# One row's gate matmuls moved from the boundary between two tiles into the middle of the second

## What is computed

```python
def _mixer_rglru(x, h0, conv_buf, p):
    gate_br, rnn_br = jnp.split(x @ p['w_in_c'], 2, axis=-1)
    xc, new_buf = _causal_dwconv(rnn_br, conv_buf, p['conv_w_c'], p['conv_b_c'])
    xb = xc.reshape(bsz, length, N_LRU_BLOCKS, LRU_BLOCK)
    r = sigmoid(einsum('blnc,ncd->blnd', xb, p['w_gate_a']) + p['b_gate_a'])
    i = sigmoid(einsum('blnc,ncd->blnd', xb, p['w_gate_x']) + p['b_gate_x'])
    log_a = LRU_C * r * log_sigmoid(p['lru_lambda'])
    a = exp(log_a)
    b = sqrt(-expm1(2.0 * log_a)) * (i * xc)
    _, h = associative_scan(_linear_combine, (a, b), axis=1)
    y = gelu(gate_br) * h
    return y @ p['w_out_c'], h[:, -1], new_buf
```

## Time and profile before

| what | value |
|---|---|
| median of 3 runs | 1378.18 us |
| lowest, highest | 1377.60, 1379.18 us |
| profiled execution, its own time | 1379.3 us |
| its span, first to last instruction | 1377.5 us |
| PE, DVE, ACT, POOL busy | 1354.0, 957.2, 721.3, 137.7 us |

### The profile page before, as it was taken

How to read it: one execution, slowest core, us unless ns; L and a number is a source line. 1 busy time by engine, 2 the same in 40 slices (tenths; PEclk the granted TensorE clock), 3 DMA queues, 4 the chain that set the end, 5 groups by cost and what they waited for, 6 DMA issues and landing times.

```text
span 1377.5 us, 24827 instructions
## 1 busy us (share of the span) xinstructions
PE 1354.0 (98%) x9860; PEld 1328.7 (96%) x9860; DVE 957.2 (69%) x1499; ACT 721.3 (52%) x1129; POOL 137.7 (10%) x146
## 2 busy tenths in 40 slices
PE   7999999999999999999999999999999999999996
PEld 7999999999999999999999999999999999999996
DVE  5657566565788658844886778888884688448865
ACT  5443544453565347722764568755652467236734
POOL 0020111100230000000000330022400000000002
PEclk9999999999999999999999999999999999999998
DMA  8165587849812345533554259853498855335522
GB/s 313 62 227 190 138 191 190 255 105 286 220 59 69 89 130 161 169 95 100 162 163 141 77 187 209 227 133 103 141 222 234 247 161 176 92 115 161 169 62 85
DMA packets 80899, 217.47 MB, mean 158 GB/s; under 512 B 6928, under 2 KB 9232, under 8 KB 80528
## 3 DMA queue, kind: packets, MB, share of 16 engines
q1 hardware_dynamic: 52704, 138.95, 30.9%
q0 software_dynamic: 27648, 76.03, 22.7%
q10 hardware_dynamic: 432, 0.91, 0.2%
HBM read 208.23 MB, written 74.74 MB: 205 GB/s over the span
## 4 chain that ended last, share of the span: by engine, by line
PE 87%; DVE 7%; ACT 3%; DMA 1%; issue 1%; SPq 0%; DVEq 0%; ACTq 0%
PE PS L781 27%; PE PS L782 26%; PE PS L783 26%; DMA raw<-weights 1%; PE PS L950 1%; PE PS L959 1%; DVE Y L1891 1%; PE PS L965 1%; PE PS L909 1%; DVE Y L1879 1%; PE PS L930 1%; DVE S L2220 1%; PE PS L939 1%; PE PS L1096 0%; DVE wlo L1598 0%
## 5 line engine op out<-in xcount | busy, mean ns | idle before, releaser
L781 PE MATMUL PS<-xhi,whi 128*128 128x296 f32 (+1 forms) x1536 | 470.3, 306 | 7.8 <-DVE wlo L1604 7.6
L782 PE MATMUL PS<-xlo,whi 128*128 128x296 f32 (+1 forms) x1536 | 458.8, 299 | 0.0
L783 PE MATMUL PS<-xhi,wlo 128*128 128x296 f32 (+1 forms) x1536 | 458.5, 298 | 0.0
L1130 ACT ACTIVATE whi<-raw 128x1024 fp32r<-128x1024 f32 (+2 forms) x256 | 254.3, 995 | 198.7 <-PE PS L783 192.9
L1598 DVE TENSOR_TENSOR wlo<-raw,whi 128x1024 fp32r<-128x1024 f32 (+2 forms) x256 | 294.2, 1152 | 64.9 <-ACT whi L1130 55.6
L781 PEld LDWEIGHTS PS<-xhi,whi 128*128 128x128 f32 x1536 | 290.9, 189 | 10.8 <-issue 8.2
L782 PEld LDWEIGHTS PS<-xlo,whi 128*128 128x128 f32 x1536 | 291.4, 190 | 1.4
L783 PEld LDWEIGHTS PS<-xhi,wlo 128*128 128x128 f32 x1536 | 290.4, 189 | 0.0
L781 PE MATMUL PS<-hhi,whi 128*128 128x296 f32 (+2 forms) x864 | 258.1, 299 | 0.4 <-DVE Y L1816 0.4
L782 PE MATMUL PS<-hlo,whi 128*128 128x296 f32 (+2 forms) x864 | 256.9, 297 | 0.0
L783 PE MATMUL PS<-hhi,wlo 128*128 128x296 f32 (+2 forms) x864 | 256.2, 297 | 0.0
(11 more groups left out here) (268 smaller groups left out, 1674.5 us busy)
## 6 DMA issues: line engine op xcount, KB each, us to landing
raw<-weights SPq DMA_DIRECT2D x118, 512.0 KB, 4.3
weight_sums<-weights POOLq DMA_DIRECT2D x24, 2048.0 KB, 16.7
raw<-weights SPq DMA_DIRECT2D x100, 256.0 KB, 3.3
weight_sums<-weight_sums POOLq DMA_DIRECT2D x8, 2048.0 KB, 10.6
raw<-weight_sums SPq DMA_DIRECT2D x64, 256.0 KB, 3.4
raw<-weight_sums SPq DMA_DIRECT2D x32, 512.0 KB, 4.1
raw<-weights SPq DMA_DIRECT2D x16, 384.0 KB, 3.3
Y<-xT SPq DMA_DIRECT2D x8, 296.0 KB, 10.6
```

The lines of the kernel that those rows point to most:

```text
L781: pe.matmul(dst, wh, h, start=first, stop=False, skip_group_check=onto)
L782: pe.matmul(dst, wh, lo, start=False, stop=False, skip_group_check=onto)
L783: return pe.matmul(dst, wl, h, start=False, stop=last, skip_group_check=onto)
L1130: act.activation(high(u, i)[:, 0:n], raw_of(u, i), ACT.Copy).then_inc(w_hi, 1)
```

## The change

The gates of the eighth row (m = 7) leave `GATES_AFTER`, where they stood behind index 13. `GATES_WITHIN` names index 14, k step 3 and row 7: `gemm` for index 14 is given a side function that issues `gates(7)` behind the fourth k step, so 24 of the tile's matmuls stand in front of the gates and 24 behind. `GATES_READ` is written so that its entry for index 14 is again row 7. No instruction is added or removed.

```diff
-GATES_AFTER = {3: (0, 1), 5: (2,), 6: (3,), 9: (4,), 10: (5,), 12: (6,), 13: (7,)}
-GATES_READ = {i if i == 3 else i + 1: rows for i, rows in GATES_AFTER.items()}
+GATES_AFTER = {3: (0, 1), 5: (2,), 6: (3,), 9: (4,), 10: (5,), 12: (6,)}
+GATES_WITHIN = (14, 3, 7)
+GATES_READ = {i if i == 3 else i + 1: rows for i, rows in GATES_AFTER.items()} | {GATES_WITHIN[0]: GATES_WITHIN[2:]}
...
+            def gates_within(u, k):
+                if k == GATES_WITHIN[1]:
+                    gates(GATES_WITHIN[2])
+
             first_tiles(U_RNN, 1)
             pe.wait_ge(gw_loaded, 16)
             for i in range(3, len(MIXER)):
-                gemm(U_RNN + i, xhi, xlo)
+                gemm(U_RNN + i, xhi, xlo, side=gates_within if i == GATES_WITHIN[0] else None)
                 for m in GATES_AFTER.get(i, ()):
                     gates(m)
```

## The result

| kernel | median of 11 runs | lowest, highest |
|---|---|---|
| before | 1378.19 us | 1377.60, 1380.68 us |
| after | 1381.58 us | 1379.31, 1382.50 us |

The ratio is 1.0017 with a 95% interval of 1.0009 to 1.0024: slower by about 2.3 us, inside the 0.2% that I had called no change, but outside the measurement's own uncertainty. The forecast was +0.66 us. The ratio compares means; the medians lie further apart, 3.4 us (1.0025), because the runs of after fall into two groups and the median lies in the upper one. That median, 1381.58, is 0.3 above the upper end of my range; 1378.18 times the ratio, 1380.5, lies inside it, but above 1380.2, where the range of my sum alone had ended.

A forecast was written before the change was run, and what follows sets the result against it. TensorE, busy 98%, was taken to bound the kernel, with a chain from the eighth row's gates to accumulator 0 ending equally late. +0.73 - 0.07 = +0.66 us on 1378.18 gave 1378.8 us, range 1377.4 to 1381.3.

The forecast's parts named there:

- (a): Before the fifteenth tile: TensorE's wait goes, as the tile's own needs are already met; gain 2.36 us.
- (b): Eighth row's gates inside the fifteenth tile: start 0.83 us later, end 0.73 late; 0 to 0.4 extra for their place.
- (c): After the gates, the tile's other half and the sixteenth tile: TensorE free at 908.91, 2.47 us earlier.
- (d): ScalarE and VectorE chain behind the gates: 0.73 us later, so the output projection starts at 912.21 after a 3.30 us wait.
- (e): Second output tile: the sixteenth tile's gelu follows the other at once, so a wait of 0.07 us is saved.
- (f): Output pair's seventh k step, needing the fourth pair of recurrent rows: both ends move 0.73 us, slack of 1.7 stays.
- The sum: Whole kernel: chain delay of 0.73 us less 0.07 saved at the second output tile, +0.66 us.
- Rival 2: New pause before the output projection: the clock falls, costing up to 3.1 us, 1381.9 us; chance 0.17.
- Rival 1: Output projection: not held by accumulator 0, so TensorE keeps 1.0 us of its gain, 1377.2 us; chance 0.07.
- rival 3: Fifteenth tile's first half or the moved gates meet another wait: 1378.2 to 1381.4 us; chance 0.03.

The follow-up runs named there:

- before_look3: The kernel before, unedited, in a further profiled execution: 1379.13 us.
- k5: The changed kernel with the gates behind the sixth k step instead of the fourth: median 1382.86 us, ratio 1.0026 to the kernel before.
- fill5: The changed kernel with five unneeded f32 matmuls in the pause before the output projection: median 1379.13 us, ratio 1.0009 to the kernel before.
- before_look1: The kernel before, unedited, in another profiled execution: 1378.74 us.
- before_look2: The kernel before, unedited, in a further profiled execution: 1380.2 us.
- k2: The changed kernel with the gates behind the third k step instead of the fourth: median 1379.82 us, ratio 1.0008 to the kernel before.
- k1: The changed kernel with the gates behind the second k step instead of the fourth: median 1378.00 us, ratio 0.9995 to the kernel before.
- k2_fill3: k2 with three unneeded f32 matmuls in the pause before the output projection: median 1378.63 us, ratio 0.9998 to the kernel before.
- k3_early_w: The changed kernel with ScalarE's weight conversion for unit 17 moved ahead of its gate reads: median 1382.07 us, ratio 1.0026 to the kernel before.

## Why the prediction was right and wrong

- **(a), (b), (c)** held to 0.01 us: no pause at 894, gates 897.35, PE free at 908.92. Nothing was to be added for gates inside an accumulation (1.77 us to the next matmul in both places), the lower end of my 0 to 0.4.
- **(d)** held, in place and in size: output projection at 912.20, pause 3.1 us by records, released by the gelu. The reading that a start 0.14 us behind a gelu is a wait, though no view named it, was the one that mattered; before_look3 names the wait, and in k5 both ends of the chain move together, by 1.59 (gates) and 1.60 us (output projection).
- **(e)** held in mechanism: the gelus follow each other. The first stretch of the projection is 0.15 shorter than in the profile of before (13.28 in fill5 against 13.43), where I counted 0.07. But before_look1 and before_look3 have 13.30 and 13.27: there the gelus followed each other already, and nothing was to be saved.
- **(f)** held: no profile of after shows a wait at the seventh k step.
- **The sum**, +0.66, was a term too small. It took the delay of the gates from the one profile in which the convolution ended latest; with the two other undisturbed profiles it is 0.86 and 1.12, with nothing to take off by (e). fill5, which has the late chain and no fall, measured 1.0009 (1.0000 to 1.0018), that is 1.2 us.
- **Rival 2**, the clock, was right in mechanism, place and price (3.1 us at most; measured 1.3 to 2.8), and wrong in its chance. The failed step is "decides from a pause somewhere between the 2.2 us that were harmless and the 2.3 to 2.8 us that were not". Harmless was what one execution showed. The pause at the same place, shorter with 1.97 us, wasn't harmless in before_look2, and 2.29 us at 910 wasn't in k2. A pause of about 2 us has a chance of a fall (about 3 in 10 in before, 6 of 11 in k2), one of 3.1 a larger one (15 of the 22 runs of after have a mean clock of 0.996 or less), one of 4.7 left no execution below 1381.44. With the median of after more often than not in a disturbed group, 0.17 should have been near one half, and the likeliest time near 1380.5.
- **Rival 1** fell with (d), **rival 3** with (a).

Together: 2.3 us by the ratio. The starts put the chain at 0.6 to 1.1 us and the rest is the clock, net of the falls that before has as well and after loses with its pause at 894. The split isn't sharper than that, as the interval of fill5 alone is 2.5 us wide. That the time by the ratio lies in the stated range is owed to the room that I left toward rival 2, and so is luck as far as the sum is concerned: the range of the sum alone ended at 1380.2.

## What to carry to other kernels

Before you move work behind a wait to fill a pause, follow what that work feeds: if it leads back to the engine that paused, filling the pause with something in front of it makes the chain later and collects the pause again, larger, at the chain's end. Look for that end by starts, not by idle time, since overlapping records hid 0.1 us here. And where TensorE pauses for about 2 us or more, as it did here, count a fall of the clock with a chance, not as something that one profile rules out. Splitting the pause (k1) or filling it with matmuls that nobody needs (fill5, k2_fill3) took the falls away.

## What the runs showed of the hardware

- A fall before the output projection cost 1.3, 1.5, 2.1, 2.5 and 2.8 us in five profiles, 0.45 of the time that matmuls ran at the low level, and the same kernel has executions with none. The cost can't be told from the pause's length: 3.1 us gave 2.8 in one profile and 1.3 in another, and 4.7 us gave 2.1, since part of the low level passed in the pause.
- Matmuls that nobody needs can pay: with 2.5 us of them in a pause of 3.1 no run exceeded 1379.99, where 4 of 11 had exceeded 1382.2 (ratio 1.0009 and 1.0018, intervals that overlap).
- The same convolution ended between 10.05 and 10.67 us after the same point of PE's program over all profiles, and between 10.09 and 10.67 in the four of the kernel before: a scatter of 0.6 us in one 10 us stretch, which the total time hides.
- A table load of 1.28 us that nobody wrote ran ahead of the square root's wait for DVE in before and behind it in k3_early_w. Moving an unrelated instruction changed this and cost more than the move could gain: the output projection came 0.68 us later, where 1.06 us had been taken off its chain.
